# Four input projections of a hybrid decoder block: seven half-size products in place of eight

## The reference, cut to what matters

```
mod = silu(c) @ w_ada + b_ada                  # 6 rows of D: shift, scale, gate, twice
h   = rmsnorm(x) * (1 + sc1) + sh1
..., s_b, s_c, s_x, g_a, g_b = split(h @ w_in)
y_b = (s_b * causal_conv3(s_c * s_x)) @ w_proj_b
y_a = gated_delta_rule(q, k, v, ...) @ w_proj_a
merged = sigmoid(g_a) * y_a + sigmoid(g_b) * y_b
x   = x + gt1 * (merged @ w_out);  then a mixture of experts, then rmsnorm
```

## Time and profile before

| | us |
|---|---|
| median of 3 runs | 2002.7 (2001.5 to 2002.86) |
| the profiled execution, whole | 1999.94 |
| span of its profile | 1998.2 |
| mean granted TensorE clock | 0.985 |

### The profile page before, as it was taken

The page is one execution under the profiler, slowest core; times in us unless marked ns, Lnnn a source line. Parts: engine busy times, 40 slices in busy tenths (PEclk is TensorE's granted clock), DMA queues, the critical chain, the costliest instruction groups (busy, mean ns, idle before and its releaser), DMA issues.

```text
span 1998.2 us, 28045 instructions
## 1 busy us (share of the span) xinstructions
PE 1938.0 (97%) x9687; PEld 1613.2 (81%) x9687; DVE 1344.8 (67%) x1786; ACT 941.5 (47%) x1279; POOL 222.5 (11%) x179
## 2 busy tenths in 40 slices
PE   6999999999999999999999899997999999999996
PEld 5788888888888888888888777886888888888883
DVE  6545453111658568577585556567999999999996
ACT  5211111111444525535445243214788887878863
POOL 0000000000111021021110100001222122222210
PEclk7999999999999999999999999997999999999998
DMA  8242423211323222232231669437999999999966
GB/s 312 67 130 74 147 73 102 81 63 63 101 71 86 72 72 81 67 98 69 71 86 61 208 221 295 140 104 290 372 377 381 381 381 386 384 384 382 401 257 257
DMA packets 220504, 382.11 MB, mean 191 GB/s; under 512 B 49909, under 2 KB 162982, under 8 KB 194982
## 3 DMA queue, kind: packets, MB, share of 16 engines
q1 hardware_dynamic: 202566, 333.89, 47.9%
q10 hardware_dynamic: 8672, 30.76, 4.0%
q0 software_dynamic: 9216, 16.80, 2.2%
HBM read 348.50 MB, written 49.67 MB: 199 GB/s over the span
## 4 chain that ended last, share of the span: by engine, by line
PE 73%; DVE 12%; DMA 6%; issue 4%; ACT 3%; SPq 1%; DVEq 0%; ACTq 0%; POOLq 0%
PE ps L710 33%; PE ps L2774 17%; PE ps L2818 8%; PE ps L2669 4%; PE ps L2760 1%; DVE vv L1706 1%; DVE qk L1706 1%; DMA inv_rows<-inv_d 1%; DMA inv_d<-sub_x 1%; DVE LX L1883 1%; DVE pair_prod L1781 1%; PE ps L2573 1%; PE ps L2603 1%; PE ps L2798 1%; PE ps L2617 1%
## 5 line engine op out<-in xcount | busy, mean ns | idle before, releaser
L605 DVE TENSOR_TENSOR mw_lo<-mw_raw,mw_hi 128x2048 fp32r<-128x2048 f32 x192 | 436.7, 2289 | 44.3 <-ACT mw_hi L600 44.0
L710 PE MATMUL ps<-h_hi,w_lo 128*128 128x512 f32 x1152 | 462.0, 401 | 0.5 <-DVE h_lo L1571 0.5
L710 PE MATMUL ps<-h_hi,w_hi 128*128 128x512 f32 x1152 | 449.2, 390 | 0.0
L710 PE MATMUL ps<-h_lo,w_hi 128*128 128x512 f32 x1152 | 448.7, 389 | 0.0
L600 ACT ACTIVATE mw_hi<-mw_raw 128x2048 fp32r<-128x2048 f32 x192 | 368.1, 1919 | 116.2 <-PE ps L2774 67.0
L710 PEld LDWEIGHTS ps<-h_hi,w_hi 128*128 128x128 f32 x1152 | 216.2, 188 | 45.8
L710 PEld LDWEIGHTS ps<-h_hi,w_lo 128*128 128x128 f32 x1152 | 216.8, 188 | 40.8 <-DVE h_lo L1571 0.6
L710 PEld LDWEIGHTS ps<-h_lo,w_hi 128*128 128x128 f32 x1152 | 216.8, 188 | 39.3
L671 DVE TENSOR_TENSOR w_lo<-w_raw,w_hi 128x1024 fp32r<-128x1024 f32 x88 | 107.6, 1223 | 155.4 <-ACT w_hi L666 154.2
L2774 PE MATMUL ps<-mw_hi,xT_lo 128*128 128x512 f32 x512 | 204.1, 399 | 3.0 <-DVE xT_lo L2206 2.3
L2774 PE MATMUL ps<-mw_hi,xT_hi 128*128 128x512 f32 x512 | 201.1, 393 | 0.0
(11 more groups left out here) (402 smaller groups left out, 3072.1 us busy)
## 6 DMA issues: line engine op xcount, KB each, us to landing
mw_raw<-in_w_dram SPq DMA_DIRECT2D x192, 1024.0 KB, 8.4
w_raw<-in_w_in_dram SPq DMA_DIRECT2D x72, 512.0 KB, 4.1
ada_b<-in_w_ada_dram SPq DMA_DIRECT2D x8, 2048.0 KB, 7.9
y_t<-y_d SPq DMA_DIRECT2D x7, 1024.0 KB, 10.1
ada_sc<-in_w_ada_dram SPq DMA_DIRECT2D x4, 1024.0 KB, 8.7
w_raw<-in_w_proj_b_dram SPq DMA_DIRECT2D x8, 512.0 KB, 4.2
merged_b_d<-sc_y ACTq DMA_DIRECT2D x8, 512.0 KB, 2.6
decay<-crow_d SPq DMA_DIRECT2D x8, 512.0 KB, 5.9
```

The costliest lines, as they stand in the source:

```text
L605: dve.tensor_tensor(mw_lo[off % NSPLIT][:], mw_raw[off % NRAW][:], mw_hi[off % NSPLIT][:], ALU.subtract).then_inc(mw_lo_done, 1)
L710: last = pe.matmul(dst, lhs[:, s, k], rhs[:, k, cols], start=(k == 0 and part == 0), stop=(k == KD - 1 and part == 2))
```

## The change

Two column tiles of a projection, by two halves of the inputs (4 blocks each), are a 2 x 2 block matrix; so is h (two halves of its channels by two halves of the tokens). The product of such matrices is made as seven half-size products in place of eight, on sums of blocks, and the results are added up in PSUM's and SBUF's blocks afterwards.

- Iteration i = 0 keeps whole tiles, four of them (g_b is now here). Iterations 1 to 7 are two pairs each: (s_c, s_x) and (s_b, g_b). Pair q has seven products of 4 blocks x 3 parts = 12 matmuls, in the order B11, T2, T1, T3, B21, T4, B22, in three banks (`seven_products`).
- POOL makes the weight sums, four subtractions of 128 x 512 for a pair (`weight_sums`); ACT and DVE split seven operands of 128 x 512. For h, POOL and DVE make 16 blocks of sums of 128 x 512 once, and they are split.
- After the products DVE does seven additions and two multiplications of 128 x 512 for a pair (`pair_dve`), and in the first pair of an iteration the three taps. T3, T4 and B22 wait for counts of `combined`, since their banks still hold a product.
- s and sigmoid(g_b) go to DRAM (`s_d`, `gate_b_d`) and come back. The region of `s_hi` and `s_lo` now holds the sums of h until the last pair is done.
- The product with w_proj_b is a stage "proj_b" of 8 tiles after all pairs. The late rows of mod are moved here: 16 chunks of 256 columns in two buffers, two for each tile. `mod_turn` is now ahead of the first `key_products`.

Its core:

```diff
-    phases = (("conv", 8, (0, 1, 2), 0), ("gate_b", 8, (0, 1), 0), ("first", 1, (0, 1), 0),
+    phases = (("conv", 1, (0, 1, 2, 1), 0), ("proj_b", 4, (0, 1), 0), ("first", 1, (0, 1), 0),
               ("head", 8, (0, 1, 2, 0, 1), 2), ("merge", 4, (0, 1), 0))
+    PAIR_LOADS = 2 * 7
...
+            top_, low = slice(0, HALF), slice(HALF, T)
+            pool.wait_ge(h_lo_done, past(KD))
+            for k in range(KH):
+                raw = sums_raw[k % 2]
+                if k >= 2:
+                    pool.wait_ge(h_lo_done, past(KD + k - 1))
+                pool.tensor_tensor(raw[:, 0], h_sum[k][:, low], h_sum[k + KH][:, low], ALU.add).then_inc(operand_sums, 1)
+                pool.tensor_tensor(raw[:, 2], h_sum[k][:, top_], h_sum[k][:, low], ALU.subtract).then_inc(operand_sums, 1)
+            def weight_sums(i, w):
+                q = 2 * i - 2 + w
+                f1, f2 = pair_w[w]
+                pool.wait_ge(w_in_sem[w], 32 * i + 16 * w + 16)
+                if isinstance(q, int) and q == 0:
+                    pool.wait_ge(proj_done, group("conv", 0, 0, 1))
+                else:
+                    pool.wait_ge(op_lo_done, 7 * (q - 1) + T4 + 1)
+                pool.tensor_tensor(w_sums[0][:], f2[:, 0:KH], f1[:, 0:KH], ALU.subtract).then_inc(operand_sums, 1)
+                pool.wait_ge(operand_sums, 2 * KH + 4 * q + 1)
+                pool.tensor_tensor(w_sums[1][:], f2[:, KH:], w_sums[0][:], ALU.subtract).then_inc(operand_sums, 1)
+                pool.tensor_tensor(f2[:, 0:KH], f2[:, KH:], f2[:, 0:KH], ALU.subtract).then_inc(operand_sums, 1)
+                pool.wait_ge(operand_sums, 2 * KH + 4 * q + 2)
+                pool.wait_ge(op_lo_done, 7 * q + T1 + 1)
+                pool.tensor_tensor(w_sums[0][:], f1[:, KH:], w_sums[1][:], ALU.subtract).then_inc(operand_sums, 1)
...
-            def load_ada(i):
-                ada_col = (4 + i) * 4 * P if isinstance(i, int) else sp.snap((4 + i) * 4 * P)
-                sp.wait_ge(ada_used, 3 + i)
-                sp.dma_start(ada_b[:], w_ada_d[:, :, bass.ds(ada_col, 4 * P)]).then_inc(ada_in[2], 16)
-            sp.wait_ge(x_normed, TT)
-            sp.wait_ge(ada_in[2], 16 * 3)
-            load_ada(0)
-            with sp.Fori(1, KD) as i:
-                for p, col in enumerate(CONV_COLS):
-                    load_w(sp, "conv", i, p, w_in_d, i * P + col)
-                load_ada(i)
...
+            def load_ada(i, n):
+                col = i * (4 * P) + (16 * P + n * 2 * P)
+                col = sp.snap(col) if not isinstance(col, int) else col
+                if not (isinstance(i, int) and i == 0):
+                    sp.wait_ge(ada_used, 2 * i + n + 2)
+                    sp.sem_inc(waits_passed, 1)
+                sp.dma_start(ada_h[n][:], w_ada_d[:, :, bass.ds(col, 2 * P)]).then_inc(ada_in[n], 16)
+            def load_pair(i, w):
+                for f in range(2):
+                    col = i * P + ((CONV_COLS[0], CONV_COLS[1]), (CONV_COLS[2], GB0))[w][f]
+                    col = sp.snap(col) if not isinstance(col, int) else col
+                    sp.dma_start(pair_w[w][f][:], w_in_d[:, :, bass.ds(col, P)]).then_inc(w_in_sem[w], 16)
...
+            def load_s(k):
+                if k == 0:
+                    sp.wait_ge(conv_step, TT + SC_TAPS * KD)
+                if k in (2, 3):
+                    sp.wait_ge(seventh_mm, 7 * PAIRS - 7 + k)
+                if k >= 4:
+                    sp.wait_ge(op_lo_done, 7 * PAIRS + k - 3)
+                sp.wait_ge(s_out, 16 * (k + 1))
+                sp.dma_start(s_raw[k % 4][:], s_d[k * P:(k + 1) * P, :]).then_inc(tile_in[k % 4], 16)
...
+            sp.wait_ge(combined, 4 + 9 * PAIRS)
+            sp.wait_ge(mb_out, past(16 * KD))
+            for n in range(2):
+                load_ada(0, n)
+            with sp.Fori(1, KD // 2) as i:
+                for p in range(2):
+                    load_w(sp, "proj_b", i, p, w_b_d, i * (2 * P) + p * P)
+                    sp.wait_ge(mb_done, past(4 * i + 2 * p - 2))
+                    sp.sem_inc(waits_passed, 1)
+                    load_gate(i, p)
+                    for n in range(2):
+                        load_ada(2 * i + p - 1, n)
+            for n in range(2):
+                load_ada(KD - 1, n)
...
+            def copy_first(i, w):
+                q = 2 * i - 2 + w
+                act.wait_ge(seventh_mm, 7 * q + 1)
+                if not isinstance(q, int) or q >= 1:
+                    act.wait_ge(combined, 4 + 9 * (q - 1) + 8)
+                act.activation(first_p[:], ps[:, SETS[w][0]], ACT.Copy).then_inc(sc_copied, 1)
+            def send_s(i):
+                act.dma_start(s_d[bass.ds(i * P, P), :], sc_acc[:]).then_inc(s_out, 16)
+            def second_gate(i, srcs):
+                act.wait_ge(mb_out, past(16 * i))
+                for n, src in enumerate(srcs):
+                    act.activation(gate_sig[:, n * HALF:(n + 1) * HALF], src, ACT.Sigmoid).then_inc(gb_sig, 1)
+            def send_gate(i):
+                act.wait_ge(gb_sig, past(2 * i + 2))
+                act.dma_start(gate_b_d[bass.ds(i * P, P), :], gate_sig[:]).then_inc(mb_out, 16)
+            def gated_pair(i):
+                act.wait_ge(combined, 4 + 18 * i)
+                send_s(i)
+                second_gate(i, (u2[:], c22[:]))
+                send_gate(i)
+            def pair_act(i, w, send=True):
+                copy_first(i, w)
+                for o in range(7):
+                    operand_hi(act, *after(i, w), o)
+                    if o == 0 and w == 0 and send:
+                        gated_pair(i - 1)
...
+            def pair_dve(i, w, lows=True, between=()):
+                q = 2 * i - 2 + w
+                a, b, c = SETS[w]
+                steps = 4 + 9 * q
+                following = after(i, w)
+                def low(*which):
+                    for o in which:
+                        if lows:
+                            operand_lo(dve, *following, o)
+                def combine(out, bank, other, mm):
+                    dve.wait_ge(seventh_mm, 7 * q + mm)
+                    dve.tensor_tensor(out[:], ps[:, bank], other[:], ALU.add).then_inc(combined, 1)
+                low(0)
+                dve.wait_ge(sc_copied, past(2 + q + 1))
+                if w == 0:
+                    dve.wait_ge(gb_sig, past(2 * i))
+                combine(u2, b, first_p, 2)
+                low(1, 2)
+                dve.wait_ge(combined, steps + 1)
+                combine(u3, b, u2, 4)
+                dve.wait_ge(combined, steps + 2)
+                combine(c22, c, u3, 4)
+                combine(u2, c, u2, 4)
+                for step in between:
+                    step()
+                low(3, 4)
+                combine(first_p, a, first_p, 5)
+                if w == 0:
+                    combine(u3, b, u3, 6)
+                    low(5)
+                    dve.wait_ge(combined, steps + 4)
+                    combine(u2, c, u2, 7)
+                    dve.wait_ge(combined, steps + 7)
+                    dve.tensor_tensor(prod[:, SC_TAPS - 1:SC_TAPS - 1 + HALF], first_p[:], u2[:], ALU.mult)\
+                       .then_inc(combined, 1)
+                    dve.tensor_tensor(prod[:, SC_TAPS - 1 + HALF:], u3[:], c22[:], ALU.mult).then_inc(combined, 1)
+                    low(6)
+                    dve.wait_ge(combined, steps + 9)
+                    conv_taps(i)
+                else:
+                    dve.wait_ge(conv_step, CS + SC_TAPS * i + SC_TAPS)
+                    dve.wait_ge(combined, steps + 5)
+                    dve.tensor_tensor(sc_acc[:, 0:HALF], first_p[:], sc_acc[:, 0:HALF], ALU.mult).then_inc(combined, 1)
+                    combine(u3, b, u3, 6)
+                    dve.wait_ge(combined, steps + 7)
+                    dve.tensor_tensor(sc_acc[:, HALF:], u3[:], sc_acc[:, HALF:], ALU.mult).then_inc(combined, 1)
+                    low(5)
+                    combine(u2, c, u2, 7)
+                    low(6)
...
+            def proj_b_dve(i, p, following):
+                tile = 2 * i + p
+                for n in range(2):
+                    dve.wait_ge(ada_in[n], 16 * tile + 64)
+                    for k in range(KD):
+                        ada_add(ada_h[n], 2 * tile + n + 2, k)
+                dve.wait_ge(mb_out, past(16 * tile + 16 * KD))
+                dve.wait_ge(mb_arrived[p], 16 * i + 16)
                 for n in range(2):
                     cols = slice(n * HALF, (n + 1) * HALF)
...
+                    dve.wait_ge(proj_done, group("proj_b", i, p, n))
+                    dve.tensor_tensor(sc_acc[:, cols], ps[:, 2 + 2 * p + n], gate_in[p][:, cols], ALU.mult)\
+                       .then_inc(mb_done, 1)
+                split_w_lo(dve, *following)
...
+            def seven_products(i, w):
+                q = 2 * i - 2 + w
+                a, b, c = SETS[w]
...
+                    pe.wait_ge(combined, 4 + 9 * (q - 1))
```

(99 more changed lines are left out.)

421 lines of the change are left out of this document (254 added, 167 removed).

## The result

The changed kernel takes 2032.3 us (2030.2 to 2034.6, 4 runs) where the kernel before takes 2002.8: a ratio of 1.0159, 95% interval [1.0147, 1.0171]. The forecast was 2022 with a range of 2001 to 2044. The profiled execution has a span of 2029.5 against 1998.2, and all but 2.4 of these 31.3 us have come by the first key products: they start at 545.96, before at 517.1. Of all executions reported here, one (of e10_loads_only) took 6773 us where its nine others took 1990 to 1999; it is left out of that kernel's ratio.

A forecast was written before the change was run, and what follows sets the result against it. The prediction took PE's matmuls as the bound up to 501 us. Key products 17.4 us later plus 2.6 for a slower clock, +20 us on 2002.7, gave 2022 us, range 2001 to 2044.

The forecast's parts named there:

- Part 1: Matmuls of the changed stages: 1752 in place of 1920, 168 fewer at 0.2268 us each, worth 38.1 us.
- Part 2: Way into the pairs: they begin at 100.5 us, and PE waits 3.7 us for pair 0's first addition.
- Part 3: Pairs: POOL's additions delay DVE, T3 waits about 1.3 us in 7 second pairs, 8.5 us allowed; pairs end at 380.7.
- Part 4: The proj_b tiles, where the loss was expected: 16.35 us a tile where PE needs 10.9; eighth multiply ends at 516.8.
- The ring: In proj_b, each multiply waits for folds, which wait for loads, which wait for the multiply before; 16.35 us a round.
- P: Period of a proj_b tile: issue 0.15, loads 7.0, two folds 7.8, two multiplies 1.4, together 16.35 us.
- M0: End of the first proj_b multiply, put 21.6 us after the pairs end: last sigmoid's store, chunk load, folds, multiply.
- Part 5: After the last multiply: key products 17.7 us later, at 534.5, 17.4 later than before; slower clock then costs 2.6 us.
- Rival (a): In proj_b, loads and folds fit in PE's 10.9 us a tile, so the kernel takes about 1982 us; chance 0.12.
- (b): In proj_b, the circle of waits exists but is short, 13.5 to 14.6 us: 1998 to 2009 us; chance 0.10.
- (c): POOL holds DVE longer in the pairs, or slow clock makes proj_b tiles up to 21.8 us: 2040 to 2060; chance 0.13.
- (d): The change doesn't remove the 168 matmuls, and proj_b's circle of waits still costs: 2060 us; chance 0.01.

The follow-up runs named there:

- e10_loads_only: Changed kernel with only two SP order changes: chunk loads ahead of the wait for the multiply, weights of stage first ahead of the last chunk loads; 1994.1 us.
- e5: Changed kernel with DVE's three taps moved behind the next pair's first addition; 2028.3 us.
- e6: Changed kernel with POOL's weight sums from the third pair on made on 8 columns only (output not the reference's); 2025.8 us.
- e1: Changed kernel with SP issuing a proj_b tile's chunk loads ahead of its wait for the multiply and of the gate load; 2000.3 us.
- e4: Changed kernel with the w_ada chunks loaded once and folded eight times in place, 14 of 16 chunk loads left out; 1983.7 us.
- e2: Changed kernel with DVE multiplying each proj_b tile between its two chunk folds, not behind both; 2009.8 us.
- e3: Changed kernel with the two weight loads of stage first issued ahead of the last two chunk loads; 2022.9 us.
- e8: Changed kernel with chunk loads first, multiply between folds, first weights ahead of last chunks, taps later, mod rows after the key products; 1986.2 us.

## Why the prediction came out as it did

- **Part 1 is right.** PE ran 168 matmuls fewer. One of the pairs costs a little more than the 0.2268 taken: in e5 and e6 888 of them take 203.0 us, 0.2286 each. Over 1176 that is 2.1 us.
- **Part 2 is right but for its size.** The pairs begin at 100.2 (predicted 100.5), and the wait ahead of the first T3 is 2.3 (3.7), for the first addition, as predicted. The 16 sums of h are hidden. A cost that no term has: right behind this wait PE runs at the lower clock (0.57 from 111 to 115 us), which makes some eight matmuls cost about 0.43 us each, 1.6 us in all.
- **Part 3: the mechanism is right, its size partly luck.** An iteration takes 39.6 us (212.46 to 252.06 and on), where 168 x 0.2286 is 38.4: 1.2 us at each second T3, 1.3 predicted. The cause is POOL beside DVE, as e6 shows. But the wait is shorter in the first two iterations (0.5 and 1.0) and absent in the last, where POOL makes no sums: by the starts of the matmuls it is 5.6 us in all, not 8.5. The pairs end at 372.75 + 3 x 2.72 = 380.9 (380.7) because two waits that were priced too high (together by some 4 us) pay for the dearer matmuls (2.1) and the lower clock (1.6), which were priced at nothing.
- The rule by which two engines exclude each other for a whole instruction (the Trainium skill, "SBUF — State Buffer", "Who interferes with whom") agrees with the two ends in e6's comparison above. Of rows 8, with which the prediction bore it out, only the product of 2.11 us has two SBUF inputs; the step of 1.10 is of the other kind that the last section names. The rule's other half, that an instruction with one SBUF input is spared, agrees too: this addition out of PSUM starts in the middle of a POOL sum, and costs no more than alone:

```profile
109.48 1.73 POOL L847 TENSOR_TENSOR pair_w<-pair_w 128x512 f32<-128x512 f32 x1
110.00 0.68 DVE L1841 TENSOR_TENSOR comb<-ps,comb 128x512 f32<-128x512 f32 x1
```

- **Part 4: the mechanism is right, one of its terms was too small.** The ring holds the stage (e1 and e4 break it, e2 shortens it), DVE waits for loads, SP for the multiplies. But the first six steps average 17.3 us where P was 16.35: + 5.8 us. The folds are as predicted (0.35 + 3.61) and so are the multiplies (1.3). The mis-sized term is the first, 0.15 us from the multiplies to the issue: the gate load and the next waits stand on SP ahead of the chunk, which begins 0.93 us after the multiplies end (438.47 to 439.40), and then takes 6.95. M0 is 2.0 late (404.34 against 402.3): the store of the last sigmoid lands 8.9 us after T0 and not 6.8, since the sigmoids (383.35) stand on ACT behind the split of the fifth reload of s, and the store takes 5.41 us (384.42 to 389.83).
- The sentence that the period "doesn't hold PE at all" was wrong in every second tile. The second chunk's load also waits until PE has summed the chunk that its buffer held (L2631), and that sum stands behind half a tile of 24 matmuls. In the chain above, from 412.11, this path and the one of two folds in a row end within 0.3 us of each other. It also runs through PE at the lower clock: PE had just stood idle for 4.8 us (411.46 to 416.27), and the 24 matmuls take 7.84 us in a tile with a granted clock of 0.83, against 5.57 in e1 at 1.00.
- **A term was missing: the last tile.** Its step is 21.7 us, 5.4 over P, since the weights of "first" stood on SP behind a chunk load that waits for PE, and DVE's split of them ahead of both folds. The prediction named the weights queued behind DVE's waits, but not those queued behind SP's. e3 removes it.
- **Part 5 is nearly right.** Key products at the end of M7 + 16.0 (17.7), silu's end at + 12.9 (14.2). After them the kernel loses 2.4 us more than the one before (2.6 predicted), with a granted clock of 0.72 in the first 10 us, where the kernel before had 1.00. PE had been idle for 5.6 us just ahead of them (10 predicted).
- **The sum.** 2.0 + 5.8 + 5.4 - 1.7 = 11.5 us later than the predicted 534.5: 546.0. Rival (a) fell by its own test, multiplies 17 us apart and not 11; (b) too. Of (c), the clock did fall, to 0.83 and 0.97 by turns, but tiles are 17 us, not 21.8. (d) fell with the count of matmuls. e4 (1983.7, with loads left out) and e8 (1986.2, with the other edits as well) come near the 1982 of (a), but no kernel with only the ring cut does: e1 took 2000.3, its tiles 12.4 us and not the 10.9 that (a) took, its last step 19.6.

## What to carry to other kernels

Before work is moved onto an engine's idle time, write down each queue's order around it, SP's too, and follow every load back to the wait that stands ahead of it: a load, a fold and a multiply that wait for each other in a circle have a period of their own, however idle the DMAs and the engines are. A load that needs only its buffer shouldn't stand behind a wait for something else: here two moved blocks of issue code (e10) were worth 38 us of the 46 won, as much as all the matmuls that the change saves. Follow the ring to the last round too, where the next stage's loads come in with other waits ahead of them.

## What the runs showed of the hardware

- POOL can hold DVE up for more than its share: with two POOL sums in a row, a DVE multiplication of 0.69 us took 1.20 and the next 1.78, while POOL's second sum went from 1.29 to 1.74. For DVE that is 1.6 us more for both; I had taken 1.9.
- A step with one SBUF input can be held as well: in e8 a tap of 128x512, 0.48 us at its place with POOL idle, took 2.33 from 489.35 on, and ended 0.29 us after POOL's addition (488.98 + 2.41 = 491.39). The addition out of PSUM was not held (0.68 at 110.00, beside POOL's sum from 109.48). The same section of the Trainium skill's "SBUF — State Buffer" counts such tensor-scalar steps, in a two-port mode, among those that contend.
- A chunk of 1 MB, read in pieces of 1 KB behind 0.5 MB in the same queue, landed 7.4 us after its issue (median of 16), against 7.9 for 2 MB in 2 KB pieces and 5.2 to 5.4 for one with little beside it (389.89; 511.08 in e3). In e1 the same chunks went at 280 GB/s in place of 214: it is the time to land, not the rate, that the ring pays.
- In tiles of 17 us in which PE was busy for 12 to 15 it was granted 0.83 and 0.97 by turns. With the loads moved, the same matmuls ran at 1.00 (e1). The lower clock was no matter of PE's own time only: half a tile at 7.84 us stood on a path of the ring.
